# The opening of a hybrid decoder step on one core: identity made on the chip, sample rows on another queue, transposes moved into the first tile

## The reference, cut to what matters

```python
h = rmsnorm(x, attn_norm_w)
proj = h @ w_in              # 1024 x 6400: xin, Bg, Cg, q, k, v, g_conv, g_attn
y_conv = Bg * causal_short_conv(Cg * xin, prefix, conv_w)
y_attn = window_attention(rmsnorm(q), rmsnorm(k), v)      # window 128, 16 heads, 2 kv heads
x = x + (sigmoid(g_conv) * y_conv + sigmoid(g_attn) * y_attn) @ w_out
x = x + moe(rmsnorm(x))      # top 4 of 32 experts, each 1024 -> 2048 -> 1024
```

## Time and profile before

| | |
|---|---|
| median of 3 runs | 1146.74 us (1146.21 to 1146.78) |
| the profiled execution | 1146.49 us, span of its trace 1144.7 us |
| TensorE busy | 1096.0 us, 96% of the span |
| VectorE, ScalarE, GpSimd busy | 39%, 17%, 8% |
| memory traffic | 444.38 MB, mean 388 GB/s |
| granted TensorE clock, mean | 0.993 |

### The profile page before, as it was taken

One profiled execution on the slowest core, in us unless ns is written; L12 is line 12 of the kernel. 1 busy time (PEld: TensorE's weight loads), 2 busy tenths in 40 slices (PEclk: granted clock), 3 DMA queues, 4 the chain that ended last, 5 costly groups with the idle time before them and its releaser, 6 DMA issues.

```text
span 1144.7 us, 15230 instructions
## 1 busy us (share of the span) xinstructions
PE 1096.0 (96%) x6125; PEld 503.9 (44%) x6125; DVE 441.5 (39%) x864; ACT 190.5 (17%) x405; POOL 88.7 (8%) x161
## 2 busy tenths in 40 slices
PE   9999999999999999999899999999999999999997
PEld 6889898543333333333333333333333333333333
DVE  6578786652433323233222222323232323232322
ACT  3233341221321101010101010101010101010101
POOL 1775215000000000000000000000000000000000
PEclk9999999999999999999999999999999999999999
DMA  9937529999999999999999999999999999999996
GB/s 317 320 119 212 184 86 370 418 368 416 402 418 435 415 432 430 435 428 435 427 434 434 428 435 428 435 427 435 434 427 436 428 434 428 435 433 429 427 423 270
DMA packets 53206, 444.38 MB, mean 388 GB/s; under 512 B 13100, under 2 KB 19372, under 8 KB 35740
## 3 DMA queue, kind: packets, MB, share of 16 engines
q1 hardware_dynamic: 46712, 435.83, 91.6%
q0 software_dynamic: 5600, 7.32, 2.4%
q10 hardware_dynamic: 852, 0.64, 0.2%
HBM read 439.78 MB, written 2.37 MB: 386 GB/s over the span
## 4 chain that ended last, share of the span: by engine, by line
PE 62%; DMA 37%; DVE 0%; issue 0%; ACT 0%; ACTq 0%; SPq 0%; DVEq 0%
PE pA L2115 33%; DMA ring<-in_w_up 21%; PE pB L2115 20%; DMA ring<-in_w_down 10%; PE pM L2115 6%; DMA area<-in_w_up 5%; PE pM L2118 1%; PE pA L2118 1%; DMA x<-in_x_prompt 1%; ACT area L1327 0%; DVE x L1961 0%; SPq L848 0%; DVE conv_row L1875 0%; DVE x L2042 0%; ACTq L1109 0%
## 5 line engine op out<-in xcount | busy, mean ns | idle before, releaser
L2115 PE MATMUL pA<-ring,hn 128*64 128x512 f32 x1536 | 352.7, 602 | 23.9 <-DMA ring<-in_w_up 23.8
L2115 PEld LDWEIGHTS pA<-ring,hn 128*64 128x64 f32 x1536 | 105.3, 137 | 219.5 <-issue 185.4
L2115 PE MATMUL pB<-ring,area 128*64 128x512 f32 (+3 forms) x784 | 169.2, 582 | 6.5 <-DMA ring<-in_w_down 5.7
L2115 PE MATMUL pA<-area,hn 128*64 128x512 f32 x512 | 119.3, 609 | 10.4 <-DMA area<-in_w_up 10.4
L2115 PE MATMUL pB<-area,ring 128*128 128x132 f32 (+3 forms) x896 | 119.6, 313 | 0.6 <-DVE tmp L1453 0.5
L2115 PEld LDWEIGHTS pB<-area,ring 128*128 128x128 f32 (+1 forms) x896 | 105.0, 179 | 14.1 <-issue 2.5
L2115 PEld LDWEIGHTS pB<-ring,area 128*64 128x64 f32 (+2 forms) x784 | 58.8, 136 | 98.3 <-issue 85.9
L1961 DVE TENSOR_TENSOR x<-pM,x 128x512 f32<-128x512 f32 x60 | 40.1, 692 | 147.6 <-PE pM L2115 147.6
L1315 ACT ACTIVATE area<-area 128x512 f32<-128x512 f32 x30 | 19.0, 632 | 386.2 <-DVE area L1944 386.2
L1875 DVE COPY conv_row<-pM 128x512 f32<-128x512 f32 x30 | 20.6, 686 | 146.8 <-PE pM L2115 146.8
L2115 PEld LDWEIGHTS pA<-area,hn 128*64 128x64 f32 x512 | 36.0, 139 | 74.5 <-issue 59.5
(11 more groups left out here) (351 smaller groups left out, 918.1 us busy)
## 6 DMA issues: line engine op xcount, KB each, us to landing
ring<-in_w_up SPq DMA_DIRECT2D x36, 4096.0 KB, 29.8
ring<-in_w_down SPq DMA_DIRECT2D x18, 4096.0 KB, 29.2
area<-in_w_up SPq DMA_DIRECT2D x12, 4096.0 KB, 30.2
ring<-in_w_up SPq DMA_DIRECT2D x16, 2048.0 KB, 12.7
area<-in_w_down SPq DMA_DIRECT2D x6, 4096.0 KB, 30.1
ring<-in_w_in SPq DMA_DIRECT2D x22, 1024.0 KB, 9.6
ring<-in_w_down SPq DMA_DIRECT2D x16, 1024.0 KB, 10.2
ring<-in_w_up SPq DMA_DIRECT2D x16, 1024.0 KB, 8.3
```

Source lines behind the costliest of these rows:

```text
L2115: return pe.matmul(out, w, m, start=start, stop=stop, skip_group_check=True)
```

## The change

Six things are done at once.

- `ident` is no longer loaded. GpSimd clears it, waits for itself, and sets the diagonal to one with an `affine_select`.
- The sample rows move from SyncE's queue to GpSimd's, behind that select and ahead of the convolution state.
- On SyncE's queue the second half of x tile 0 moves behind the first half of the k and v weights.
- TensorE turns the first halves of x ahead of "anorm", and the second halves inside tile 0, after its product 1 (function `turns`).
- The warm-up has 7 products instead of 12.
- VectorE's two squares of x tile 0 move behind the first half of `weighted`; ScalarE's square of the sample rows moves between the two `raw_columns`.

```diff
         def _(sp):
             sp.dma_start(x[:, 0, 0:512], x_prompt[0, 0:128, 0:512]).then_inc(x_loaded[0][0], 16)
-            sp.dma_start(x[0:DEC, 2, :], x_sample.rearrange("b t d -> (b t) d")).then_inc(x_sample_loaded, 16)
-            sp.dma_start(x[:, 0, 512:D], x_prompt[0, 0:128, 512:D]).then_inc(x_loaded[0][1], 16)
             for n, (dst, src) in enumerate(w_in_chunk(0)):
                 sp.dma_start(dst, src).then_inc(kv_loaded[n], 16)
+                if n == 0:
+                    sp.dma_start(x[:, 0, 512:D], x_prompt[0, 0:128, 512:D]).then_inc(x_loaded[0][1], 16)
...
         def _(pool):
+            nc.gpsimd.memset(ident, 0.0).then_inc(ident_cleared, 1)
+            pool.wait_ge(ident_cleared, 1)
+            nc.gpsimd.affine_select(out=ident, in_=ident, pattern=[[-1, 128]], compare_op=ALU.not_equal, fill=1.0,
+                                    base=0, channel_multiplier=1).then_inc(ident_made, 1)
+            pool.dma_start(x[0:DEC, 2, :], x_sample.rearrange("b t d -> (b t) d")).then_inc(x_sample_loaded, 16)
             pool.wait_ge(cleared, 1)
...
-            act.dma_start(ident, consts[:, C_ID:C_ID + 128]).then_inc(ident_loaded, 16)
...
-            act.wait_ge(x_sample_loaded, 16)
-            nc.scalar.activation(hn[0:DEC, 2, :], x[0:DEC, 2, :], ACT.Square, accum_out=stat[0:DEC, 2:3])
...
             raw_columns(0)
+            act.wait_ge(x_sample_loaded, 16)
+            nc.scalar.activation(hn[0:DEC, 2, :], x[0:DEC, 2, :], ACT.Square, accum_out=stat[0:DEC, 2:3])
             raw_columns(1)
...
-                    squared(0)
                     dve.wait_ge(x_halves, 1)
                     weighted(0, 4, 0, 128, pA[:, 0:512]).then_inc(raw_dve, 1)
+                    squared(0)
                     ins = squared(1)
...
-            keep_busy(zeros[:, 0:128], zeros, 12)
-            pe.wait_ge(ident_loaded, 16)
-            pe.wait_ge(anorm_loaded, 16)
+            def turns(h):
+
+                for m in range(2):
+                    pe.wait_ge(x_loaded[m][h], 16)
+                    for k in range(4 * h, 4 * h + 4):
+                        o = 1024 * m + 128 * k
+                        mm = tr(pA[:, o:o + 128], x[:, m, 128 * k:128 * k + 128])
+                    mm.then_inc(x_halves, 1)
+
+            keep_busy(zeros[:, 0:128], zeros, 7)
+            pe.wait_ge(ident_made, 1)
             for what, a in STEPS:
                 if what == "anorm":
+                    turns(0)
+                    pe.wait_ge(anorm_loaded, 16)
                     tr(misc_bank()[:, 0:KT], rows[V_ANORM:V_ANORM + KT, :]).then_inc(misc_full, 1)
...
                     for k in range(KT):
                         if c == 0:
+                            if a == 0 and k == 2:
+                                turns(1)
```

More of the change, by code:

```diff
@@ L262 @@
 V_TURNED, K_TURNED, CACHE_TURNED, QUERIES_MOVED, CONV_TURNED = 1, 2, 3, 4, 5
-TURNS = [(0, 0), (1, 0), (0, 1), (1, 1)]
 RAW_TILES = 2
@@ L562, in build @@
         x_sample_loaded = sem("x_sample_loaded")
-        ident_loaded = sem("ident_loaded")
+        ident_made = sem("ident_made")
+        ident_cleared = sem("ident_cleared")
         consts_loaded = sem("consts_loaded")
@@ L2217, in _ @@
                     mm.then_inc(misc_full, 1)
-                    for m, h in TURNS:
-                        pe.wait_ge(x_loaded[m][h], 16)
-                        for k in range(4 * h, 4 * h + 4):
-                            o = 1024 * m + 128 * k
-                            mm = tr(pA[:, o:o + 128], x[:, m, 128 * k:128 * k + 128])
-                        mm.then_inc(x_halves, 1)
                 elif what == "rstd":
```

## The result

The changed kernel takes 1152.03 us (median of 6 runs, 1150.36 to 1152.48), the kernel before 1146.76 (6 runs beside them). The ratio is 1.0044, with a 95% interval of 1.0033 to 1.0054: slower by about 5 us. The forecast was 1155.7, range 1146.2 to 1160.3. Its largest term was wrong, a smaller one came out right in size, and one was missing.

What follows compares the result with a forecast made beforehand. TensorE, busy 96% of the span, was taken to bound the kernel from the first tile's start on. Later start 6.0 plus longer tile 3.0 made 9.0 us on 1146.49, so 1155.5, median 1155.7; range 1146.2 to 1160.3.

Steps and rivals of the forecast that it cites:

- The identity: GpSimd's making of the identity, a 6.0 us code load included, would have it ready at 7.3 us.
- the price of the library's load: Fetching GpSimd's code for the select from memory: 6.0 us taken, bounds from nothing to 8.3.
- The select itself: GpSimd's select that sets the identity's diagonal: 0.3 us taken, bounds 0.1 to 1.0.
- The sample rows: Ordered on GpSimd's queue at 7.3, landing at 13.3; the first tile starts at 15.05, 6.0 us later.
- B: Rival: no load to speak of, the clock comes up; 1148.0, or 1146.5 to 1147.0 with faster sample rows; chance 0.22.
- Tile 0: Transposes and ScalarE's columns inside the first tile: plus 1.3 us at 2.4 GHz, plus 3.0 at the low level, taken.
- its clock term: TensorE begins the first tile's work at the low level: 6.8 us for the tile instead of 5.1.
- a pause of 3.1 us up to the identity: TensorE stands still from the warm-up's end at 4.2 until 7.3, so it begins real work at the low level.
- C: Rival: no load, but seven warm-up matmuls don't bring the clock up; tile plus 3.0, start unchanged, 1149.7; chance 0.12.
- Weights earlier, worth nothing: First k and v weights land at 7.5 to 8.1 instead of 8.96; no gain, the tile waits for the sample rows.
- Squares and state rows: ScalarE's square of the sample rows (1.04) is covered; state loads issued behind the sample rows cost nothing.
- All shifts reach the end: TensorE runs without a gap from the first tile, so a microsecond there is a microsecond at the end.

Runs made afterwards that it cites:

- e2: The changed kernel with the sample rows' transfer back on SyncE's queue, as its second, and seven warm-up products: 1149.86 us, ratio 1.0027.
- e12: The changed kernel with the identity loaded again on ScalarE's queue, no memset or select on GpSimd, and twelve warm-up products: 1147.82 us, ratio 1.0008.
- e5: The changed kernel with twelve warm-up products, plus five zero products ahead of and five behind the sample rows' transposes: 1149.94 us, ratio 1.0027.
- e3: The changed kernel with the second halves' eight transposes ahead of the first tile, behind the sample rows': 1150.00 us, ratio 1.0031.
- e10: The kernel before with the sample rows first on GpSimd's queue and the second halves of x turned inside tile 0: 1148.98 us, ratio 1.0017.
- e6: The kernel before with seven warm-up products instead of twelve, nothing else: 1147.74 us, ratio 1.0005.
- e1: The changed kernel with twelve warm-up products instead of seven, all else as changed: 1150.54 us, ratio 1.0036.
- e4: The kernel before with the identity cleared and selected by GpSimd instead of loaded, nothing else: 1147.60 us, ratio 1.0008.
- e9: The kernel before, identity transfer kept, plus a GpSimd memset and select into a spare array that nothing reads: 1146.85 us, ratio 0.9997.
- e7: The kernel before with the sample rows moved to GpSimd's queue as its first item, nothing else: 1146.95 us, ratio 1.0002.
- e11: The kernel before with the second half of x tile 0 ordered behind the first half of the k and v weights: 1147.05 us, ratio 1.0005.

## Why the prediction was right in direction and too high

**The identity: wrong, 6.0 us too much.** The step that failed is the price of the library's load, "I take 6.0, because code has to come from memory". The row of after has 0.24 us between memset and select. The nearest rows that I had bounded it with ranged from 0 to 8.3, and the choice inside that range rested on no row. The 6 us that the Trainium skill gives for a first call into freshly loaded code (GPSIMD Engine Reference, section 2.1 Instruction dispatch) did not appear here; the measurement decides. The select itself (0.3 taken, 0.28 measured) was right.

**The sample rows: the place right, its size 1.0 under, its start 5.6 over.** I had them ordered at 7.3 and landing 6.0 us later; it was 1.72 and 7.0. They set the start of the tile, as predicted: the chain runs through them and e2 removed them from it. Of the range named for this transfer, 1.8 to 8.3, the row of the same queue in the same stretch (6.0) was the near one; the 2.0 us plus the bytes of the Trainium skill's DMA: Bandwidth & Descriptors (Anatomy of one DMA, SWDGE) was not seen in any of the seven kernels that order the rows on this queue (4.4 to 7.0). From landing to tile it took 2.3 us, not 1.75: the eight small transposes ran at the low level, 1.04 for 0.64. So the start moved by 1.9 instead of 6.0. This is the mechanism of B, whose rows at 6.0 us gave a start of 9.05; it was short by 0.4 in the order, 1.0 in the landing and 0.5 behind it.

**Tile 0: right in size, plus 3.0; its clock term partly by luck.** Working at the low level: 6.8 us predicted, 6.67 measured. At the high level 5.1 predicted, 5.17 and 5.18 in e12 and e5. The split is 1.5 for the transposes and ScalarE's columns inside the tile, with e3 and e10 in agreement, and 1.5 for the clock in the changed kernel's trace. The reason given for the low clock, a pause of 3.1 us up to the identity, was not the one that came: the transposes followed the warm-up within 0.2 us and ran at the low level all the same, and the first long pause, 2.09 us for the sample rows, came after them. That is C's mechanism, seven products that don't bring the clock up, with a later start; C, at 1149.7, had the start unchanged. But it does not come every time: e2's seven brought it up by 4.51, and e6's cost something in half of its runs. In e1's trace the pauses undid a longer warm-up, in e5's, with the pauses filled, the clock held, and in e12's it held over a pause of 1.20. What makes one execution of a kernel keep its clock and another lose it is open.

**Weights earlier, worth nothing: right.** They landed at 1.24 + 4.4 = 5.64, still earlier than the 7.5 to 8.1 forecast, and waited over 5 us for the tile. Squares and state rows: no wait for them is in the list of after.

**All shifts reach the end: right.** 4.9 at the tile's end, 4.7 at the last TensorE instruction, and within 0.7 us in all rows of the table.

**The tail: missing.** I followed the change only as far as TensorE. The identity's transfer was one of ScalarE's queue, and without it the kernel ends 0.7 to 1.1 us later behind TensorE's last instruction. Seven kernels without the transfer have a tail of 6.2 to 6.3, seven with it 5.2 to 5.5, whatever else they differ in. ScalarE's two last orders take 0.95 or 0.96 us in all of the former and 0.67 to 0.69 in all of the latter. e4 against e9 rules out GpSimd's work, and e12, which takes the transfer back into the changed kernel, has the short tail again; so it goes with the missing transfer. How one 64 KB transfer at the start reaches the stores at the end, 1140 us later, is open: the traces show a later second order and a later landing, and no run parts the number of that queue's transfers from their size. They do hold one lead. Queue q14 carries transfers of the kind "instruction", 8 KB each. In the seven kernels with the identity's transfer one of these falls at 1089 to 1092 us, shown here by the queues' view of the trace before, 1080 to 1100 us (packets, MB, share):

```profile
q14 instruction: 1, 0.01, 0.1%
```

In the seven without it there is none between 337 and 1143 us, and three instead of two fall behind that. So ScalarE's list, shorter by one order, may be fetched in other pieces, of which one is now due while the last stores are ordered. No run tests this.

**The sum.** Predicted 6.0 + 3.0 = 9.0. Measured 1.9 (start) + 3.0 (tile) - 0.2 (given back on the way) + 0.95 (tail) = 5.7 in the traces, 5.3 in the medians. So the start was put 4.1 us too high and the tail left out. The direction holds without the load, since the tile's 3.0 and the late rows are losses by themselves; that the load was counted in did not help it. The range, 14 us wide, reached from no load at all to one of 8.3 us, so that the result fell inside says little. All rivals lacked the tail: C with it comes to 1150.7, 1.4 below the median where the forecast is 3.7 above.

**Could the change be made to win?** Nothing here beat the kernel before. With the identity loaded and twelve products (e12) the change gives 1147.82, since the tile cannot start before the first columns are weighted, and every transpose behind that point is on the path. e7, e9 and e11 show that three parts are free by themselves, within the interval: the sample rows first on GpSimd's queue, the memset and select, and the order of x and weights. Not run were these parts with all transposes ahead of the tile and the identity loaded, the squares' new place alone, and VectorE weighting its half of token tile 0 ahead of the sample columns.

## What to carry to other kernels

Work that fills the time in which another engine prepares the next step is free where it stands and costs its full length where it is moved to; before moving it, ask what bounds the start that it is meant to free (here the first weighted columns, at 9.3 in e10 and 8.5 in e12). A transfer put behind another engine's work can be late by more than that work (1.1 to 3.0 us for 0.44 here), and what follows it can lose as much again through TensorE's clock (1.5 us in the changed kernel's trace, 2.3 in e1's). Follow a removed transfer to the end of its queue, and look at both ends of the trace: 0.9 of 5.7 us lay in the last six microseconds.

## What the runs showed of the hardware

- GpSimd's first select came 0.24 us behind a memset and took 0.28 for 128x128.
- A 32 KB transfer on GpSimd's queue landed 4.4 to 5.1 us after its order at 1.28, and 5.8 to 7.0 after its order at 1.72.
- How soon the clock comes up differs between executions: behind seven warm-up products eight transposes took 1.06 us in e2, 1.52 in e3 and 1.94 in the changed kernel.
- A pause of TensorE does not decide on the clock by itself. After 1.39 us without work the tile of e10 ran at 1.2 GHz. In e9 TensorE had nothing between 8.0 and 9.6 us, and the windows there show the high level:

```profile
9.00:10.00 1.00, 0.38 (x3) 0.38 (x4) 0.21 (x1) 0.00 (x0) 0.00 (x0) 1.00 1.12 313
10.00:12.00 2.00, 2.00 (x12) 1.74 (x11) 0.00 (x0) 1.68 (x6) 0.00 (x0) 1.00 1.10 343
```

- At the start of a trace the granted clock can read 1.00 while the issues are those of the low level (the changed kernel's tile, 0.44 us between issues of 264 columns; its window from 10 to 12 us is below). There the distance of the issues is the measure.

```profile
10.00:12.00 2.00, 1.02 (x3) 0.84 (x4) 1.90 (x6) 0.00 (x0) 0.00 (x0) 1.00 1.10 348
```

- The same transfer lands over a microsecond earlier or later in traces of kernels that order it alike: the second half of x tile 1 took 6.0 us in the trace of before, 7.3 in e9's and 6.8 in e6's. The start of the tile in one trace is no measure of an edit that is worth less; the medians are.
